# Suffix sums of a stick-breaking attention as single-pass products of a split softplus, and the adaptive units placed anew

## The chip, the cores and the metric

One core of one Trainium2 chip runs the whole kernel. The metric is device time in microseconds. Before the change three runs took 1232.63, 1235.06 and 1237.28 us, with a median of 1235.06 us. TensorE (PE in the rows; PEld is its weight load), VectorE (DVE), ScalarE (ACT), GpSimd (POOL) and SyncE (SP, which here only issues DMAs) each run a queue of instructions in order and meet at semaphores.

## The reference, cut to what matters

The kernel computes two transformer blocks on 256 tokens of width 1024. The first block is an adaptive normalisation (six vectors sh1, sc1, g1, sh2, sc2, g2 from a condition c and the weight ada_w), a stick-breaking attention of 16 heads, and a mixture of 32 experts. The second block is a feed-forward, a mixer and a feed-forward. The change is inside the attention:

```
mod = silu(c) @ ada_w + ada_b; sh1, sc1, g1, sh2, sc2, g2 = split(mod, 6)
h = rms_norm(x) * (1 + sc1) + sh1
z = q @ k.T * scale                       # per head, 256 x 256
log_keep = where(causal, log_sigmoid(-z), 0)   # = -softplus(z)
suffix = cumsum(log_keep, reverse=True) - log_keep
a = where(causal, exp(log_sigmoid(z) + suffix), 0)
x = x + g1 * ((a @ v) @ w_out)
h = rms_norm(x) * (1 + sc2) + sh2; x = x + g2 * experts(h)
```

## The kernel before

**Attention.** Heads go in pairs, p = 0 to 7. A head's logits lie transposed (keys on the partitions) in one of four PSUM banks, as 384 columns (three 128x128 blocks; the fourth is all masked), called BLK. `scores(p)` on TensorE fills the banks of the pair. ScalarE takes Abs, Exp and Ln of it (lines 1149 to 1151, tile `att_az`). VectorE's `softplus_head` (L1584) makes max(z, 0) plus that, into `att_sp`. GpSimd's `keep_causal` (L934) zeroes what is masked in the two diagonal blocks (256 columns). TensorE's `suffix_sums(p)` (L2426, L2427) adds two products to the bank of each head: `neg_ge` (a triangle of -1) times all 384 columns and `neg_ones` times the last 128 columns. Everything is plain fp32 there, and the profile shows such a product as two instructions. VectorE's `weight_logs` (L1612) copies min(sum, 0) to `att_a` and frees the bank, ScalarE takes Exp (L1159), GpSimd masks again (L934), and `weigh_values(p)` (L2436, L2440) multiplies by v. ScalarE rounds the result (L1163, `oTh`) and VectorE keeps what the rounding left (L1640, `oTl`).

**The split products.** The large projections do the same with weights and activations: a value is split into a rounded part (type fp32r, by ScalarE) and the rest (VectorE, rounded too), and three single-pass products take the place of one fp32 product (L2255 to L2257).

**The order.** Each engine's order is written out by hand as a loop over p. In iteration p TensorE does suffix_sums(p), weigh_values(p-1), one half of an adaptive unit where one is due (`ada`, L2311: SC2 in p = 1 and 2, SH2 in p = 3 and 4, G2 in p = 6 and 7), scores(p+2), and in p = 1 `gate_col` (L2334), in p = 3 and 5 `ada_col` (L2323). VectorE does weight_logs and softplus_head for two heads in turn, then `ada_part` (L1497) or `ada_col` (L1506), from p = 4 to 7 a half of an output weight's rest (`early_part`, L1538), then oTl.

**The weights' ring.** SyncE loads 2 MB units into six ring slots. The list `units_a` names them; unit n waits until unit n-6 is used. After the last of the list, the experts' weights take the same slots and five spare areas. They are again issued in order, each when its slot's last user is through: SH2's and G2's halves and the splits of the two output units release the first ones, the output products and the router the next, and the experts' own products all later ones (L804). `BankPlan` gives each PSUM use its bank.

Of the kernel before, what the change touches and what calls it, by code (L numbers as in the profile page):

```python
# [63 lines left out]
ADA_AT = {3: SC2, 5: SH2}  # L64
# [18 lines left out]
def plan_banks():  # L83
# [24 lines left out]
    for p in range(PAIRS + 2):  # L108
        if p < PAIRS:
            for h in (2 * p, 2 * p + 1):  # L110
                plan.use(("z", h), bank=h % 4, fills=2)
        if p >= 2:
            plan.use(("o", p - 2), bank=4 + p % 2, fills=0)
        if p in ADA_AT:
            plan.use(("ada", ADA_AT[p], None), bank=6, fills=0)
        if p == 2:
            plan.use(("col", G1, None), bank=7)
        if p - 1 in ADA_AT:
            plan.use(("col", ADA_AT[p - 1], None), bank=7)
    plan.use(("ada", G2, None), bank=6, fills=0)  # L120
# [96 lines left out]
def build_program(nc, x_in, c_in, ada_w, ada_b, norm_g, final_g, sb_w_in, sb_w_out, moe_w_grp, moe_b_grp,  # L217
# [5 lines left out]
    with ctx:  # L223
# [20 lines left out]
        def area(name, offset, *sizes, dt=FP32):  # L244

            return shaped(place(name, offset, [P, *sizes], dt)[0][:], sizes)
# [47 lines left out]
        att_a = area("att_a", REST + 17408, 4, BLK)  # L294

# [16 lines left out]
        neg_ones = gain0[:, 896:1024]  # L312
# [13 lines left out]
        neg_ge = vec[:, 1312:1440]  # L326
# [79 lines left out]
        def slot_b(n):  # L406
# [39 lines left out]
        z_log, z_sp, z_spm, z_a, z_am, z_o = (sem(n) for n in (  # L446
            "att_log", "att_sp", "att_sp_masked", "att_a", "att_a_masked", "att_o"))
# [102 lines left out]
        units_a += [("qkv", 2), ("qkv", 3), ("ada", G1, 0), ("ada", G1, 1), ("qkv", 4), ("qkv", 5)]  # L550
# [347 lines left out]
        def _(pool):  # L898
# [3 lines left out]
            for t, v in ((ident, 0.0), (neg_ge, -1.0), (lt, 1.0), (le, 1.0), (pick, 0.0), (strip, 0.0), (wrp, 0.0)):  # L902
                last = chain.step(g.memset(t, v))
            g.memset(neg_ones, -1.0).then_inc(consts, 1)
# [52 lines left out]
            for p in range(PAIRS + 1):  # L957
                if p < PAIRS:
                    for h in (2 * p, 2 * p + 1):
                        pool.wait_ge(z_sp, h + 1)  # L960
                        keep_causal(diag(att_sp[:, h % 4, :]), z_spm)
                if p >= 1:
                    for h in (2 * p - 2, 2 * p - 1):
                        pool.wait_ge(z_a, h + 1)
                        keep_causal(diag(att_a[:, h % 4, :]), z_am)
# [492 lines left out]
        def _(dve):  # L1458
# [147 lines left out]

            def weight_logs(g):

                b = await_full(dve, ("z", g), 2)
                if g >= 4:  # L1610
                    dve.wait_ge(z_o, g - 3)
                emptied(v.tensor_scalar(att_a[:, g % 4, :], b[:, 0:BLK], 0.0, None, ALU.min), ("z", g))  # L1612
# [6 lines left out]
            for h in range(2):  # L1619
                softplus_head(h)  # L1620
            value_copy(1, 1)
            for p in range(1, PAIRS + 2):
                for i in range(2):
                    if 1 <= p <= PAIRS:
                        weight_logs(2 * p - 2 + i)
                    if 1 <= p < PAIRS:
                        softplus_head(2 * p + i)
                if p in ADA_AT:
                    ada_part(ADA_PARTS.index((ADA_AT[p], None)))
                if p == 2:  # L1630
                    ada_col(ADA_PARTS.index((G1, None)))
                if p - 1 in ADA_AT:
                    ada_col(ADA_PARTS.index((ADA_AT[p - 1], None)))
                if 4 <= p < 8:
                    early_part(EARLY_QKV + (p - 4) // 2, p % 2)
                if p >= 2:
                    n = p - 2
                    b = bank(("o", n))
                    dve.wait_ge(oh_s, n + 1)
                    emptied(v.tensor_tensor(oTl[:, n, :], b[:, 0:T], oTh[:, n, :].bitcast(FP32), ALU.subtract), ("o", n))  # L1640
            def add_square(c):

                dve.wait_ge(sq2_s, c + 1)
                if c > 1:
                    dve.wait_ge(sq_sum_s, c - 1)
                v.tensor_tensor(sq_sum, sq_sum, sq2[:, c % 2, :], ALU.add).then_inc(sq_sum_s, 1)
# [551 lines left out]
        def _(pe):  # L2198
# [222 lines left out]
            def suffix_sums(p):  # L2421

                for g in (2 * p, 2 * p + 1):
                    b, s = bank(("z", g)), att_sp[:, g % 4, :]
                    pe.wait_ge(z_spm, g + 1)
                    t.matmul(b[:, 0:BLK], neg_ge, s, start=False, stop=True, skip_group_check=True)  # L2426
                    last = t.matmul(b[:, P:T], neg_ones, s[:, T:BLK], start=False, stop=True, skip_group_check=True)  # L2427
                    filled(last, ("z", g))
# [27 lines left out]
            for p in range(PAIRS + 1):  # L2456
# [8 lines left out]
                if 2 <= p + 1 < 6:  # L2465
                    ada(ADA_PARTS[4 + (p + 1) // 2][0], (p + 1) % 2)
                if PAIRS - 2 <= p < PAIRS:
                    ada(G2, p - PAIRS + 2)
                if p + 2 < PAIRS:
                    scores(p + 2)  # L2470
                if p == 1:
                    gate_col()
                if p in ADA_AT:
                    ada_col(ADA_PARTS.index((ADA_AT[p], None)))
# [475 lines left out]
```

## Time and profile before

| | |
|---|---|
| profiled execution | 1232.65 us |
| its span | 1230.9 us, 16444 instructions |
| PE, PEld | 1063.2 us (86%), 808.5 us (66%) |
| DVE, ACT, POOL | 510.0 us (41%), 414.3 us (34%), 71.6 us (6%) |
| attention loop | 103.82 to 146.94 us of the span |
| output projection, router | 146.94 to 188.46 us |
| experts | 188.46 to about 600 us |
| second block | about 600 us to the end |

A busy share over the whole span mixes stages with different limits, so the table says where each stage lies. The time outside the span is 1232.65 - 1230.9 = 1.75 us.

### The profile page before, as it was taken

What the parts mean: (1) busy time and instruction counts of PE and PEld (TensorE: products, weight loads), DVE (VectorE), ACT (ScalarE), POOL (GpSimd) and SP (SyncE); (2) the same over time, 40 slices, a digit from 0 to 9 for tenths busy, and PEclk for the clock granted to TensorE, in tenths of its full rate; (3) what the DMA queues carried; (4) which work ended last, traced back from release to release, by engine and by line L of the source; (5) the groups of instructions that cost most, each with busy time, mean ns of one, the idle gap of its engine ahead of it and who ended that gap; (6) DMA issues with size and microseconds to landing.
All of it is one profiled execution on the core that took longest, in us unless ns stands there. A gap on an engine that the chain in (4) does not pass through costs nothing.

```text
span 1230.9 us, 16444 instructions
## 1 busy us (share of the span) xinstructions
PE 1063.2 (86%) x7186; PEld 808.5 (66%) x7186; DVE 510.0 (41%) x617; ACT 414.3 (34%) x500; POOL 71.6 (6%) x101
## 2 busy tenths in 40 slices
PE   8999999765837383748899999999999999999998
PEld 6886693321313130313499998889888878999986
DVE  4544641120202020202075454466754886554544
ACT  3366741000100000000064444355645435434432
POOL 2073200000000000000010000000000310000000
PEclk9999999887878686969999999999999999999999
DMA  9899899999999999999996555455545346556530
GB/s 357 296 404 376 320 368 396 429 426 426 431 427 426 429 426 428 429 424 420 400 303 198 168 184 205 165 209 199 191 152 179 125 174 223 170 173 206 191 118 35
DMA packets 112822, 357.13 MB, mean 290 GB/s; under 512 B 8406, under 2 KB 55146, under 8 KB 98156
## 3 DMA queue, kind: packets, MB, share of 16 engines
q1 hardware_dynamic: 111116, 352.59, 74.1%
q10 hardware_dynamic: 1632, 3.45, 0.8%
q8 instruction: 59, 0.97, 0.3%
q14 instruction: 15, 0.12, 0.0%
HBM read 354.97 MB, written 1.05 MB: 289 GB/s over the span
## 4 chain that ended last, share of the span: by engine, by line
PE 66%; DMA 23%; SPq 5%; DVE 3%; ACT 1%; issue 1%; DVEq 0%; ACTq 0%
PE psum L2255 16%; PE psum L2257 16%; PE psum L2256 16%; DMA spare<-in_moe_w_gate_dram 5%; DMA spare<-in_moe_w_up_dram 5%; DMA ring<-in_moe_w_down_dram 5%; DMA spare<-in_moe_w_down_dram 4%; PE psum L2624 4%; PE psum L2672 3%; DMA ring<-in_moe_w_up_dram 2%; PE psum L2611 2%; DMA ring<-in_sb_w_in_dram 1%; SPq L785 1%; PE psum L2561 1%; PE psum L2311 1%
## 5 line engine op out<-in xcount | busy, mean ns | idle before, releaser
L2255 PE MATMUL psum<-hTh,wh_keep 128*128 128x256 f32 x800 | 225.4, 282 | 0.6 <-DVE hTl L1839 0.6
L2256 PE MATMUL psum<-hTl,wh_keep 128*128 128x256 f32 x800 | 224.7, 281 | 0.0
L2257 PE MATMUL psum<-hTh,wl_keep 128*128 128x256 f32 x800 | 224.7, 281 | 0.0
L1816 DVE TENSOR_TENSOR wl_stream<-ring,wh_stream 128x2048 fp32r<-128x2048 f32 x52 | 119.8, 2311 | 108.6 <-ACT wh_stream L1250 108.5
L1816 DVE TENSOR_TENSOR wl_keep<-ring,wh_keep 128x2048 fp32r<-128x2048 f32 x49 | 111.9, 2291 | 105.7 <-ACT wh_keep L1250 105.7
L2255 PEld LDWEIGHTS psum<-hTh,wh_keep 128*128 128x128 f32 x800 | 150.7, 188 | 0.9 <-issue 0.8
L2256 PEld LDWEIGHTS psum<-hTl,wh_keep 128*128 128x128 f32 x800 | 150.8, 188 | 0.0
L2257 PEld LDWEIGHTS psum<-hTh,wl_keep 128*128 128x128 f32 x800 | 150.7, 188 | 0.0
L1250 ACT ACTIVATE wh_stream<-ring 128x2048 fp32r<-128x2048 f32 x52 | 99.4, 1916 | 150.6 <-PE psum L2257 150.5
L2624 PE MATMUL psum<-spare,m_xT 128*32 128x512 f32 x416 | 90.3, 666 | 55.5 <-DMA ring<-in_moe_w_up_dram 30.3
L1250 ACT ACTIVATE wh_keep<-ring 128x2048 fp32r<-128x2048 f32 x49 | 93.6, 1919 | 124.4 <-PE psum L2257 124.0
L2624 PE MATMUL psum<-ring,m_xT 128*32 128x512 f32 x352 | 97.3, 664 | 13.4 <-DMA ring<-in_moe_w_up_dram 12.5
L2255 PE MATMUL psum<-wh_stream,hTh 128*128 128x512 f32 (+1 forms) x256 | 98.0, 383 | 0.8 <-DVE wl_stream L1816 0.8
L2257 PE MATMUL psum<-wh_stream,hTl 128*128 128x512 f32 (+1 forms) x256 | 96.4, 376 | 0.0
L2256 PE MATMUL psum<-wl_stream,hTh 128*128 128x512 f32 (+1 forms) x256 | 96.3, 376 | 0.0
L1772 DVE TENSOR_TENSOR m_h<-m_sg,psum 128x512 f32<-128x512 f32 x8 | 8.2, 1028 | 199.3 <-PE psum L2624 164.6
L2624 PEld LDWEIGHTS psum<-spare,m_xT 128*32 128x32 f32 x416 | 23.7, 122 | 96.6 <-issue 96.6
L2672 PE MATMUL psum<-ring,m_sg 128*32 128x512 f32 x288 | 54.9, 738 | 34.1 <-DMA ring<-in_moe_w_down_dram 17.7
L1202 ACT ACTIVATE m_xT<-psum,ccol 128x128 f32<-128x128 f32 x32 | 12.0, 456 | 179.8 <-PE psum L2567 179.8
L2255 PE MATMUL psum<-wh_stream,actTh 128*128 128x512 f32 x176 | 68.7, 390 | 0.0
L2256 PE MATMUL psum<-wl_stream,actTh 128*128 128x512 f32 x176 | 68.5, 389 | 0.0
L2257 PE MATMUL psum<-wh_stream,actTl 128*128 128x512 f32 x176 | 68.5, 389 | 0.0
(379 smaller groups left out, 1695.1 us busy)
## 6 DMA issues: line engine op xcount, KB each, us to landing
ring<-in_ffn_w_in_dram SPq DMA_DIRECT2D x44, 1024.0 KB, 7.8
ring<-in_moe_w_down_dram SPq DMA_DIRECT2D x18, 2048.0 KB, 37.9
ring<-in_w_mix_in_dram SPq DMA_DIRECT2D x32, 1024.0 KB, 6.3
spare<-in_moe_w_up_dram SPq DMA_DIRECT2D x14, 2048.0 KB, 34.8
ring<-in_ada_w_dram SPq DMA_DIRECT2D x24, 1024.0 KB, 13.9
ring<-in_moe_w_gate_dram SPq DMA_DIRECT2D x12, 2048.0 KB, 31.1
spare<-in_moe_w_gate_dram SPq DMA_DIRECT2D x12, 2048.0 KB, 38.9
ring<-in_moe_w_up_dram SPq DMA_DIRECT2D x10, 2048.0 KB, 37.2
```

Source lines behind the costliest of these rows:

```text
L785: sp.dma_start(dst[:, ks, :], ada_v[:, ks, lo:lo + NB]).then_inc(wa_in[n % RING_A], 16)
L1202: last = a.activation(m_xT[:, c, :], psum[:, 1, P * (c - 4):P * (c - 4) + P], ACT.Identity, scale=expert_cols[:, 0, c:c + 1], bias=expert_ ...
L1250: a.activation(dst, src, ACT.Copy).then_inc(split_h, 1)
L1816: v.tensor_tensor(split_half(h, wl), raw_half(h), split_half(h, wh).bitcast(FP32), ALU.subtract)\
L2255: t.matmul(dst, sh, mh, start=first, stop=False, skip_group_check=True)
L2256: t.matmul(dst, sh, ml, start=False, stop=False, skip_group_check=True)
L2257: return t.matmul(dst, sl, mh, start=False, stop=final, skip_group_check=True)
L2311: last = t.matmul(b[CAP * e:CAP * e + CAP, :], crep[:, 4 * s + i, :], w[:, i, NB * h:NB * h + NB], start=(s == 0 and i < 2), stop=(s == 1 ...
L2561: last = t.matmul(psum[:, c // 4, P * (c % 4):P * (c % 4) + P], hn[:, tt, P * c:P * c + P], m_sel[:, tt].rearrange("p e s -> p (e s)"), st ...
L2611: last = t.matmul(psum[CAP * e:CAP * e + CAP, 4 + i, :], m_xT[:, k, CAP * e:CAP * e + CAP], w[e // 2][e % 2][kk], start=(k == 0), stop=(k ...
L2624: last = t.matmul(psum[CAP * e:CAP * e + CAP, 4 + i, :], m_xT[:, k, CAP * e:CAP * e + CAP], w[e][:, k, :], start=(k == 0), stop=(k == KD - 1))
L2672: last = t.matmul(psum[CAP * e:CAP * e + CAP, 6 + half, :], m_hT[:, f, CAP * e:CAP * e + CAP], w[e][:, f, NB * half:NB * half + NB], start ...
```

## The change

The masked softplus is split: GpSimd masks `att_sp` in place as before, waits for itself, and copies all 384 columns into `att_sph` (fp32r, rounded). VectorE subtracts it from `att_sp` and writes the rest into `att_spl` (`softplus_rest`). `att_sph` lies where `att_az` lies and `att_spl` where `att_sp` lies, so nothing is added in memory. `neg_ge` and `neg_ones` become fp32r tiles. suffix_sums does four single-pass products per head in place of two fp32 ones, and waits for each part by itself. The adaptive units sit in other iterations, and in the ring's list the third pair of projection weights is loaded before the second half of G1.

```
-ADA_AT = {3: SC2, 5: SH2}
+ADA_UNITS = {0: (SC2, 0), 1: (SC2, 1), 2: (SH2, 0), 3: (SH2, 1), 5: (G2, 0), 7: (G2, 1)}
+ADA_COLS = {0: G1, 2: SC2, 4: SH2}
+        att_sph = area("att_sph", REST + 14336, 4, BLK, dt=F32R)
+        att_spl = area("att_spl", REST + 15872, 4, BLK, dt=F32R)
-        units_a += [("qkv", 2), ("qkv", 3), ("ada", G1, 0), ("ada", G1, 1), ("qkv", 4), ("qkv", 5)]
+        units_a += [("qkv", 2), ("qkv", 3), ("ada", G1, 0), ("qkv", 4), ("ada", G1, 1), ("qkv", 5)]
 # GpSimd, for each head of pair p
-                        keep_causal(diag(att_sp[:, h % 4, :]), z_spm)
+                        m = diag(att_sp[:, h % 4, :])
+                        chain.link(g.affine_select(out=m, in_=m, compare_op=ALU.is_gt, fill=0.0, base=0,
+                                                   pattern=[[0, 2], [1, P]], channel_multiplier=-1))
+                        g.tensor_copy(out=att_sph[:, h % 4, :], in_=att_sp[:, h % 4, :]).then_inc(z_sph, 1)
 # VectorE
+            def softplus_rest(h):
+                dve.wait_ge(z_sph, h + 1)
+                v.tensor_tensor(att_spl[:, h % 4, :], att_sp[:, h % 4, :], att_sph[:, h % 4, :].bitcast(FP32),
+                                ALU.subtract).then_inc(z_spl, 1)
             for h in range(2):
                 softplus_head(h)
+            for h in range(2):
+                softplus_rest(h)
             value_copy(1, 1)
             for p in range(1, PAIRS + 2):
                 for i in range(2):
                     if 1 <= p <= PAIRS:
                         weight_logs(2 * p - 2 + i)
                     if 1 <= p < PAIRS:
+                        if i:
+                            softplus_rest(2 * p)
                         softplus_head(2 * p + i)
-                if p in ADA_AT:
-                    ada_part(ADA_PARTS.index((ADA_AT[p], None)))
-                if p == 2:
-                    ada_col(ADA_PARTS.index((G1, None)))
-                if p - 1 in ADA_AT:
-                    ada_col(ADA_PARTS.index((ADA_AT[p - 1], None)))
+                if p - 1 in ADA_COLS:
+                    ada_col(ADA_PARTS.index((ADA_COLS[p - 1], None)))
+                if p in (2, 4):
+                    ada_part(ADA_PARTS.index((ADA_COLS[p], None)))
                 ... early_part (p = 4 to 7), oTl as before
+                if p < PAIRS:
+                    softplus_rest(2 * p + 1)
 # TensorE
-                    b, s = bank(("z", g)), att_sp[:, g % 4, :]
-                    pe.wait_ge(z_spm, g + 1)
-                    t.matmul(b[:, 0:BLK], neg_ge, s, start=False, stop=True, skip_group_check=True)
-                    last = t.matmul(b[:, P:T], neg_ones, s[:, T:BLK], start=False, stop=True, skip_group_check=True)
+                    b = bank(("z", g))
+                    for part, ready in ((att_sph, z_sph), (att_spl, z_spl)):
+                        s = part[:, g % 4, :]
+                        pe.wait_ge(ready, g + 1)
+                        t.matmul(b[:, 0:BLK], neg_ge, s, start=False, stop=True, skip_group_check=True)
+                        last = t.matmul(b[:, P:T], neg_ones, s[:, T:BLK], start=False, stop=True,
+                                        skip_group_check=True)
                     filled(last, ("z", g))
-                if 2 <= p + 1 < 6:
-                    ada(ADA_PARTS[4 + (p + 1) // 2][0], (p + 1) % 2)
-                if PAIRS - 2 <= p < PAIRS:
-                    ada(G2, p - PAIRS + 2)
+                if p in ADA_UNITS:
+                    ada(*ADA_UNITS[p])
+                elif p in ADA_COLS:
+                    ada_col(ADA_PARTS.index((ADA_COLS[p], None)))
                 if p + 2 < PAIRS:
                     scores(p + 2)
-                if p == 1:
+                if p == 0:
                     gate_col()
-                if p in ADA_AT:
-                    ada_col(ADA_PARTS.index((ADA_AT[p], None)))
+                elif p in ADA_UNITS and p in ADA_COLS:
+                    ada_col(ADA_PARTS.index((ADA_COLS[p], None)))
```

## Rows read from the trace of the kernel before

**Rows 1.** The page's first line.
```profile
span 1230.9 us, 16444 instructions
```
**Rows 2.** Windows: length, each engine's busy time (instructions), granted clock, DMA share, GB/s.
```profile
103.82:146.94 43.12, 41.78 (x306) 24.44 (x304) 25.22 (x48) 30.83 (x62) 12.64 (x30) 1.00 0.85 322
188.46:560.00 371.54, 232.52 (x1633) 86.87 (x1632) 47.90 (x87) 21.27 (x46) 0.00 (x0) 0.81 1.00 425
...
138.00:140.00 2.00, 2.00 (x17) 1.08 (x19) 2.00 (x5) 1.62 (x4) 0.04 (x1) 1.00 0.06 25
...
190.00:192.00 2.00, 2.00 (x24) 0.65 (x20) 0.00 (x0) 0.01 (x1) 0.00 (x0) 1.00 0.40 119
```
**Rows 3.** Timeline of SyncE's queue: start us, issue us, what.
```profile
141.98 2.04 SPq L753 DMA_DIRECT2D ring<-in_moe_w_up_dram  x4
...
192.12 7.14 SPq L804 DMA_DIRECT2D ring<-in_moe_w_gate_dram  x4
```
**Rows 4.** Timeline of TensorE, 103 to 118 us: start, us, what, [idle before, releaser].
```profile
103.59 0.39 PE L2257 MATMUL psum<-ewh,ehTl 128*128 128x512 f32 x1
103.82 0.81 PE L2426 MATMUL psum<-att_sp,vec 128*128 128x384 f32 x2
104.46 0.38 PE L2427 MATMUL psum<-att_sp,gain 128*128 128x128 f32 x2
104.68 0.81 PE L2426 MATMUL psum<-att_sp,vec 128*128 128x384 f32 x2
...
106.52 0.70 PE L2416 MATMUL psum<-qkT 64*128 64x256 f32 x4 [0.80 <-DVE att_a L1612]
...
107.37 0.91 PE L2426 MATMUL psum<-att_sp,vec 128*128 128x384 f32 x2
...
109.30 0.65 PE L2436 MATMUL psum<-att_a,vtok 128*64 128x256 f32 x4
...
110.10 1.92 PE L2311 MATMUL psum<-ring,gain 128*32 128x512 f32 x16
111.96 0.70 PE L2416 MATMUL psum<-qkT 64*128 64x256 f32 x4
...
114.62 0.89 PE L2426 MATMUL psum<-att_sp,vec 128*128 128x384 f32 x2
```
**Rows 5.** The chain of waits, where the loop ends.
```profile
146.14 0.58 PE psum L2436 x4
146.94 0.32 PE psum L2255
```
**Rows 6.** Timelines of ScalarE and TensorE before the loop.
```profile
74.67 1.92 ACT L1094 ACTIVATE ewh<-ring 128x2048 fp32r<-128x2048 f32 x1 [3.42 <-DMA ring<-in_sb_w_in_dram]
```
```profile
79.25 0.47 PE L2255 MATMUL psum<-ewh,ehTh 128*128 128x512 f32 x1 [0.68 <-DVE ewl L1546]
```
**Rows 7.** Timeline of all engines late in the loop.
```profile
135.15 0.70 PE L2416 MATMUL psum<-qkT 64*128 64x256 f32 x4 [0.53 <-DVE att_a L1612]
...
140.74 1.22 DVE L1538 TENSOR_TENSOR ewl<-ring,ewh 128x1024 fp32r<-128x1024 f32 x1
...
140.89 1.33 POOL L934 TENSOR_SCALAR_AFFINE_SELECT att_sp<-att_sp 128x256 f32<-128x256 f32 x1 [0.52 <-DVE att_sp L1584]
```
**Rows 8.** Single tiles and lines: duration ns min/median/max, first and last start.
```profile
L934 POOL TENSOR_SCALAR_AFFINE_SELECT att_a<-att_a x16: 402/406/408, 107.3 to 144.7; 128x256 f32<-128x256 f32 x16
```
```profile
L1584 DVE SCALAR_TENSOR_TENSOR att_sp<-psum,att_az x16: 542/548/558, 100.8 to 140.3; 128x384 f32<-128x384 f32 x16
```
```profile
L951 POOL TENSOR_TENSOR gain<-gain,ring x28: 724/740/2829, 66.1 to 95.6; 128x256 f32<-128x256 f32 x28
L1546 DVE TENSOR_TENSOR ewl<-ring,ewh x11: 2291/2293/2755, 28.9 to 149.2; 128x2048 fp32r<-128x2048 f32 x11
L1538 DVE TENSOR_TENSOR ewl<-ring,ewh x4: 1215/1226/1339, 127.1 to 140.7; 128x1024 fp32r<-128x1024 f32 x4
```
**Rows 9.** GpSimd's and ScalarE's groups by shape: count, busy us, mean ns.
```profile
L915 POOL TENSOR_SCALAR_AFFINE_SELECT le<-le 128x128 f32<-128x128 f32 x1 | 0.3, 283 | 0.0
```
```profile
L1150 ACT ACTIVATE att_az<-att_az 128x384 f32<-128x384 f32 x13 | 6.8, 523 | 0.4
```

More of the change, by code:

```diff
@@ L113, in plan_banks @@
             plan.use(("o", p - 2), bank=4 + p % 2, fills=0)
-        if p in ADA_AT:
-            plan.use(("ada", ADA_AT[p], None), bank=6, fills=0)
-        if p == 2:
-            plan.use(("col", G1, None), bank=7)
-        if p - 1 in ADA_AT:
-            plan.use(("col", ADA_AT[p - 1], None), bank=7)
-    plan.use(("ada", G2, None), bank=6, fills=0)
+        if p in ADA_UNITS and ADA_UNITS[p][1] == 0:
+            plan.use(("ada", ADA_UNITS[p][0], None), bank=6, fills=0)
+        if p in ADA_COLS:
+            plan.use(("col", ADA_COLS[p], None), bank=7)
     plan.use(("perm",), bank=7)
@@ L311, in build_program @@
         spread = gain0[:, 640:896].rearrange("p (a n) -> p a n", a=2)
-        neg_ones = gain0[:, 896:1024]
+        neg_ones = area("neg_ones", gains_at + 896, P, dt=F32R)
         adp, gate_sum = gain1.rearrange("p (a n) -> p a n", a=2), gain1
@@ L325, in build_program @@
         shift_p = vec[:, 1268:1304]
-        neg_ge = vec[:, 1312:1440]
+        neg_ge = area("neg_ge", REST + 18944 + 1312, P, dt=F32R)
         strips = vec[:, 1304:1305]
@@ L445, in build_program @@
         dve_s, act_s, pool_s = sem("dve_steps"), sem("act_steps"), sem("pool_steps")
-        z_log, z_sp, z_spm, z_a, z_am, z_o = (sem(n) for n in (
-            "att_log", "att_sp", "att_sp_masked", "att_a", "att_a_masked", "att_o"))
+        z_log, z_sp, z_sph, z_spl, z_a, z_am, z_o = (sem(n) for n in (
+            "att_log", "att_sp", "att_sp_high", "att_sp_rest", "att_a", "att_a_masked", "att_o"))
         r_diff, r_exp, r_sel, r_done = sem("rt_diff"), sem("rt_exp"), sem("rt_selected"), sem("rt_done")
@@ L901, in _ @@
             g = nc.gpsimd
-            for t, v in ((ident, 0.0), (neg_ge, -1.0), (lt, 1.0), (le, 1.0), (pick, 0.0), (strip, 0.0), (wrp, 0.0)):
+            for t, v in ((ident, 0.0), (neg_ge.bitcast(FP32), -1.0), (lt, 1.0), (le, 1.0), (pick, 0.0), (strip, 0.0), (wrp, 0.0)):
                 last = chain.step(g.memset(t, v))
-            g.memset(neg_ones, -1.0).then_inc(consts, 1)
+            g.memset(neg_ones.bitcast(FP32), -1.0).then_inc(consts, 1)
             g.memset(ones, 1.0).then_inc(consts, 1)
@@ L1626, in _ @@
                     if 1 <= p < PAIRS:
+                        if i:
+                            softplus_rest(2 * p)
                         softplus_head(2 * p + i)
-                if p in ADA_AT:
-                    ada_part(ADA_PARTS.index((ADA_AT[p], None)))
-                if p == 2:
-                    ada_col(ADA_PARTS.index((G1, None)))
-                if p - 1 in ADA_AT:
-                    ada_col(ADA_PARTS.index((ADA_AT[p - 1], None)))
+                if p - 1 in ADA_COLS:
+                    ada_col(ADA_PARTS.index((ADA_COLS[p - 1], None)))
+                if p in (2, 4):
+                    ada_part(ADA_PARTS.index((ADA_COLS[p], None)))
                 if 4 <= p < 8:
@@ L2464, in _ @@
                     weigh_values(p - 1)
-                if 2 <= p + 1 < 6:
-                    ada(ADA_PARTS[4 + (p + 1) // 2][0], (p + 1) % 2)
-                if PAIRS - 2 <= p < PAIRS:
-                    ada(G2, p - PAIRS + 2)
+                if p in ADA_UNITS:
+                    ada(*ADA_UNITS[p])
+                elif p in ADA_COLS:
+                    ada_col(ADA_PARTS.index((ADA_COLS[p], None)))
                 if p + 2 < PAIRS:
                     scores(p + 2)
-                if p == 1:
+                if p == 0:
                     gate_col()
-                if p in ADA_AT:
-                    ada_col(ADA_PARTS.index((ADA_AT[p], None)))
+                elif p in ADA_UNITS and p in ADA_COLS:
+                    ada_col(ADA_PARTS.index((ADA_COLS[p], None)))
             logits = bank(("logits",))
```

## The prediction

> **What bounds the kernel now.** I read the windows first, then SyncE's queue, then the chain, then the loop's timeline. The page's span [rows 1] hides three regimes. From 188.46 to 560 us the DMA engines are full (share 1.00, 425 GB/s) while TensorE is busy 232.52 of 371.54 us: the experts' weights bound that stage [rows 2]. Ahead of it the DMA engines still starve: at 138 to 140 us (share 0.06) and, last, at 190 to 192 us (0.40) [rows 2]. The first pause ends when SyncE issues again at 141.98 us, after VectorE's last early_part; the last one when it issues at 192.12 us, released by TensorE's first products of the experts [rows 3]. From then the stream never runs dry, so its end stands at a fixed distance behind that release, and the release follows TensorE through router, output projection and attention. So what the attention loop gains or loses on TensorE comes through whole, up to the few us of pauses that are there to be used up. In the loop TensorE is busy 41.78 of 43.12 us, VectorE 25.22, ScalarE 30.83, GpSimd 12.64 [rows 2]. TensorE bounds it, and its own idle time is two waits for weight_logs to free banks, 0.80 and 0.53 us [rows 4, 7]; by the spacing of starts they cost 0.97 (106.52 against 103.82 + 1.73) and, taken likewise, 0.61 us.
>
> **The loop's ledger before.** A pair's suffix sums take 1.93 us (107.37 to 109.30), the first pair's 1.73 us (twice 104.68 - 103.82 = 0.86). An adaptive half takes 111.96 - 110.10 = 1.86 us [rows 4]. The loop runs from 103.82 to 146.94 us [rows 4, 5], 43.1 us: 1.73 + 7 x 1.92 = 15.2 us of suffix sums, 1.6 us of those two waits, and so 26.3 us for the rest (values, scores, six adaptive halves, columns), which the change moves about and doesn't shorten.
>
> **1. The products.** An fp32 product of 384 columns takes 104.46 - 103.82 = 0.64 us, one of 128 columns 104.68 - 104.46 = 0.22 us; a single-pass product of 512 columns takes 103.82 - 103.59 = 0.23 us [rows 4]. One of 384 then takes 0.75 x 0.23 = 0.17 us. A single-pass product of 128 columns is nowhere in the trace: between 0.06 us (a quarter of 0.23) and 0.22 us (no gain over fp32). I take 0.11 us, one of the two instructions that make up the fp32 product, since its weight load is as long. A head: 2 x (0.17 + 0.11) = 0.57 us for 0.96 us. With all else hidden the suffix sums are 16 x 0.57 = 9.1 us.
> The page TensorE: Matmul & The Clock Gate of the Trainium skill (section LDWEIGHTS) gives a weight load as columns over 1.2 GHz, 107 ns for 128 columns, an estimate that would put the 128-column product at 0.11 us; the spacing of the two narrow fp32 instructions, 0.22 us for both, agrees with it [rows 4].
>
> **2. The chain to the products.** Before, a head went softplus (0.55 us), mask (0.41 us), product. Now it goes softplus, mask, wait, copy, rest, product. The mask takes 406 ns for 256 columns and 283 ns for 128 [rows 8, 9]: 0.96 ns a column over 0.16 us. A one-input copy of 384 columns by that line takes 0.53 us. Bounds: 0.41 us (as the mask) and 1.02 us (two-input adds, 740 ns for 256 columns [rows 8], by the same fixed part scaled). The rest is a two-input VectorE operation: 1226 and 2293 ns for 1024 and 2048 columns [rows 8] give 1.04 ns a column over 0.16 us, 0.56 us. With about 0.1 us at each handover the chain grows by some 1.3 us a head. Per pair VectorE gets 1.1 us more and GpSimd 1.1 us more; neither is full by sum (VectorE 25.2 + 16 x 0.48 = 33 us of 43).
>
> **3. Where the rests stand in VectorE's queue.** The rest of the even head stands behind weight_logs and holds back the odd head's softplus (0.55 us [rows 8]) until GpSimd has masked and copied. The rest of the odd head stands last, behind ada_part, the 1.22 us early_part [rows 7] and oTl, which itself waits for ScalarE. TensorE waits for it in the middle of its suffix sums, and behind that wait stand weigh_values, the adaptive half and the next scores. The bank's cycle closes there: product, weight_logs, scores, ScalarE (three passes of 0.52 us a head [rows 9]), softplus.
>
> **4. The shared port.** At 140.74 us VectorE began a two-input subtraction of 1.22 us; GpSimd's mask, begun at 140.89, took 1.33 us in place of 0.41 [rows 7, 8]. It got on only when the other was through. The other way round the subtraction of 2048 columns grew from 2291 to 2755 ns beside GpSimd's adds, which grew to 2829 from 724 [rows 8]. The rests are such subtractions, and GpSimd gets 16 copies that meet them and the early parts. I let each wait for the other, to some 0.1 us before the holder's end (1.33 us beside 0.41 says so).
> The page SBUF — State Buffer of the Trainium skill (section Who interferes with whom) calls this an exclusive lock held for the full instruction; by the trace it is let go slightly before that.
>
> **5. The walk.** I put each engine's queue in order, with these durations, and walked it through. The same walk over the kernel before ends 0.1 us from 146.94. After the change the suffix sums of pairs 0 to 7 start at 103.1, 108.8, 113.7, 119.6, 125.1, 130.5, 137.5 and 141.6 us. From start to the next product they take 1.2, 1.4, 1.5, 2.0, 2.8, 3.4, 2.5 and 4.3 us, not 1.1, plus a wait of 0.9 for pair 7's first part: 19.9 us. The last pair shows how: the softplus of head 15 runs at 142.1, early_part takes the port from 142.5 to 143.6, the mask ends 144.1, the copy 144.7, the rest 145.5, and only at 145.9 does TensorE go on to weigh_values(6) and G2's last half. Up to pair 5 the loop is ahead (adaptive halves fill the bank waits, cheap products); from pair 5 on it loses that. Sum: 19.9 - 15.2 - 1.6 = +3.1 us.
>
> **6. The ring.** The third projection unit lands one 2 MB unit earlier. Now ScalarE waits for it until 74.67 us (3.42 us idle) and through VectorE TensorE until 79.25 (0.68 us idle) [rows 6]. That idle goes and the loop starts 0.7 us earlier; what is late next is TensorE itself. G1's second half lands one unit later; GpSimd's adds of it are needed by gate_col only after 103 us. -0.7 us. SC2, SH2 are used one iteration earlier, so two output units and two expert units are requested some 6 us earlier. They only lengthen the pause before 141.98 us, since the next request still waits for the last early_part, which ends at 143.7 us by the walk. Worth nothing; nor would it cost if that cover went, the bytes being the same. gate_col in iteration 0 makes VectorE wait for it once; it is in the walk. The moved bank uses cost nothing.
>
> **Sum.** +3.1 - 0.7 = +2.4 us: the loop ends at 149.3. On the profiled execution, 1230.9 + 1.75 = 1232.65 us, it makes 1235.05; on the median of the runs, 1235.06 us, which lies 2.4 us above it, 1237.5 us. I forecast 1237.5 us.
>
> **Rivals.**
> A, TensorE stays the bound: all is hidden, 9.1 - 15.2 - 1.6 - 0.7 = -8.4 us, 1226.7 us. For it: 41.78 of 43.12 us busy, engines beside it at 25 and 31 [rows 2]. Against: what counts is the chain's length, not the sums, and a pair without an adaptive half would need 1.1 + 0.8 + 0.9 = 2.8 us of TensorE, less than the 4.3 us that VectorE's own seven operations take with an early part among them.
> B, the port doesn't matter (the collision of rows 7 was chance and the engines slip past each other): the walk without port waits ends at 147.06, +0.1 us, 1235.2 us.
> C, the copy is slow: with 1.02 us the walk ends at 154.4, +7.5 us, 1242.5 us. It decides from about 0.9 us a copy (+6). For it: two-input work costs GpSimd 2.3 ns a column; against: the mask's 0.96 ns. This is the case on the slower side in full.
> D, the 128-column single-pass product saves nothing (0.22 us): 150.5, +3.6 us, 1238.7 us; what the change says about one pass would hold for the wide half only. With both the cheap ends (0.06 and 0.41 us) it is +1.5 us.
> E, the port is held to the full end of the instruction and a little past it: the walk ends at 150.6, +3.6 us, 1238.7 us. By the Trainium skill's SBUF — State Buffer page it is this one; the 1.33 us of rows 7 speaks for the earlier release.
>
> **Chances.** The forecast 0.40, A 0.15, B 0.12, C 0.13, D 0.08, E 0.12. Plus or minus 0.5% is 6.2 us, about what a measurement of this kernel can tell. A alone lies beyond it on the fast side, and not with all its chance (0.15 less 0.04): faster 0.11. C mostly (0.11) and a little of D and E with a slower copy (0.03): slower 0.14. Same 0.75. The range leaves out the far end of A and of C: 1229 to 1243.5 us.
>
> **What would show it.** The products: L2426 once per part with about 0.17 us to the next start, and 0.11 after the narrow one. The copy: one GpSimd row per head, 0.53 us alone, longer beside L1538. The walk: TensorE idle inside suffix_sums, released by the rest on VectorE, growing from pair 3 to pair 7; the last early_part ending later than 141.98. The ring: no idle at the 79.25 product. The carry: the issue at 192.12 later by what weigh_values(7) is later by, and the DMA share at 1.00 after it. The forecast is wrong if the waits for the rests stay under 0.5 us a pair (then A), if the copy takes over 0.9 us (then C), or if a gain in the loop is not seen in the issue at 192.12.

## The result, and the profile after

The changed kernel took 1239.22 us in the median of 22 runs (1235.11 to 1242.29), the one before 1234.74 us in the median of 22 runs beside it (1232.28 to 1238.47). The ratio is 1.0032, 95% interval 1.0025 to 1.0040: 4.0 us slower, 3.1 to 4.9. The forecast was +2.4 us.

The profiled execution took 1240.75 us, 8.1 us more than the one before. That one lies 2.1 us under its kernel's median and this one 1.5 us above its own, so a single pair of traces shows about twice the difference that the runs show. Effects seen in traces are told in the traces' us; what they are worth is told in ratios.

The busy times on the page of the kernel after (TensorE hardly more than before, VectorE 7.6 us and GpSimd 12.3 us more):
```profile
PE 1064.4 (86%) x7186; PEld 808.2 (65%) x7186; DVE 517.6 (42%) x633; ACT 415.0 (33%) x500; POOL 83.9 (7%) x117
```
Windows of the kernel after, columns as in [rows 2]. The first is the attention loop, the next are 2 us slices of it, the last one is the experts' stage:
```profile
102.74:153.83 51.09, 44.50 (x305) 24.85 (x303) 32.88 (x63) 30.97 (x62) 22.28 (x44) 0.87 0.81 314
120.00:122.00 2.00, 1.42 (x12) 1.01 (x12) 1.85 (x5) 1.83 (x4) 0.00 (x0) 1.00 1.06 391
122.00:124.00 2.00, 2.00 (x16) 0.76 (x16) 1.39 (x4) 1.59 (x1) 0.91 (x2) 0.50 1.04 382
124.00:126.00 2.00, 2.00 (x14) 0.24 (x6) 0.22 (x1) 1.41 (x4) 1.63 (x4) 0.65 1.10 410
...
132.00:134.00 2.00, 0.90 (x9) 0.61 (x5) 1.79 (x5) 1.94 (x6) 1.86 (x3) 1.00 1.01 410
134.00:136.00 2.00, 1.73 (x12) 1.14 (x12) 2.00 (x4) 1.94 (x5) 1.27 (x3) 0.91 0.79 332
136.00:138.00 2.00, 2.00 (x16) 0.47 (x16) 1.39 (x4) 0.98 (x3) 0.81 (x3) 0.50 0.12 49
...
144.00:146.00 2.00, 0.71 (x4) 0.31 (x3) 2.00 (x4) 0.61 (x2) 1.21 (x1) 0.97 0.00 0
146.00:148.00 2.00, 1.26 (x4) 0.99 (x4) 1.38 (x3) 0.05 (x1) 1.65 (x4) 0.50 0.64 119
...
150.00:152.00 2.00, 2.00 (x12) 0.40 (x8) 0.42 (x1) 0.23 (x1) 0.00 (x0) 0.50 1.00 422
...
199.00:560.00 361.00, 218.84 (x1550) 81.67 (x1544) 47.45 (x86) 19.79 (x42) 0.00 (x0) 0.82 1.01 427
```
The loop runs from 102.74 to 153.83 us, 51.1 us for 43.1 [rows 2]. The loop before was granted the full clock, 1.00. This one was granted 0.87: in three stretches (122 to 125, 136 to 139, 146 to 153 us) TensorE ran at the lower of its two levels, 0.50 or 1.2 GHz, each time behind slices in which it was only partly busy (1.42, 0.90 and 0.71 of 2 us). Not every such slice has a fall behind it: from 127 to 129 us TensorE was busy for 0.89 us, and the clock stayed at 1.00 until about 135.5 us. TensorE's timeline around the first fall, columns as in [rows 4]:
```profile
119.61 0.42 PE L2441 MATMUL psum<-att_sph,neg_ge 128*128 128x384 f32 x1
...
121.24 0.44 PE L2441 MATMUL psum<-att_spl,neg_ge 128*128 128x384 f32 x1 [0.58 <-DVE att_spl L1613]
...
122.86 3.17 PE L2324 MATMUL psum<-ring,gain 128*32 128x512 f32 x16
...
129.02 0.44 PE L2441 MATMUL psum<-att_spl,neg_ge 128*128 128x384 f32 x1 [1.13 <-DVE att_spl L1613]
...
133.98 0.44 PE L2441 MATMUL psum<-att_sph,neg_ge 128*128 128x384 f32 x1 [1.10 <-POOL att_sph L964]
...
136.22 3.31 PE L2324 MATMUL psum<-ring,gain 128*32 128x512 f32 x16
```
A wait of 0.58 us for the odd head's rest, and the adaptive half behind it takes 3.17 us instead of 1.92 [rows 4]. After the waits of 1.13 and 1.10 us the next half takes 3.31 us. The loop's end, a timeline of all engines:
```profile
144.64 1.21 DVE L1541 TENSOR_TENSOR ewl<-ring,ewh 128x1024 fp32r<-128x1024 f32 x1
144.79 1.33 POOL L962 TENSOR_SCALAR_AFFINE_SELECT att_sp<-att_sp 128x256 f32<-128x256 f32 x1 [1.13 <-DVE att_sp L1587]
...
146.18 0.50 POOL L964 CAST att_sph<-att_sp 128x384 fp32r<-128x384 f32 x1
...
146.74 0.69 PE L2441 MATMUL psum<-att_sph,neg_ge 128*128 128x384 f32 x1 [1.93 <-POOL att_sph L964]
```
and the chain of waits behind it:
```profile
148.30 1.05 PE psum L2452 x4
...
149.78 3.33 PE psum L2324 x16
153.10 0.58 PE psum L2452 x4
...
153.90 0.32 PE psum L2268
```
The last early_part holds the port, GpSimd's mask takes 1.33 us, then come copy and rest, and everything that TensorE does behind them runs at 0.50: weigh_values 1.05 us for 0.58, the last half of G2 3.33. SyncE's queue afterwards, columns as in [rows 3]:
```profile
145.88 2.07 SPq L753 DMA_DIRECT2D ring<-in_moe_w_up_dram  x4
...
199.10 0.46 SPq L804 DMA_DIRECT2D ring<-in_moe_w_gate_dram  x1
```
The issue that starts the experts' stream moved from 192.12 [rows 3] to 199.10 us, +6.98, as the loop's end moved from 146.94 [rows 5] to 153.90, +6.96. From there the DMA engines are full (1.01).

### The profile page after: what moved, and what is told of

Its sections match the earlier page's. It is cut to its first block, busy times and chain, and to the rows that moved or that the text cites. A ratio compares the mean times of both kernels' runs of the same rounds, so it can differ in the third digit from the quotient of the medians.

```text
span 1238.9 us, 16476 instructions
## 1 busy us (share of the span) xinstructions
PE 1064.4 (86%) x7186; PEld 808.2 (65%) x7186; DVE 517.6 (42%) x633; ACT 415.0 (33%) x500; POOL 83.9 (7%) x117
## 3 DMA queue, kind: packets, MB, share of 16 engines
HBM read 354.97 MB, written 1.05 MB: 287 GB/s over the span
## 4 chain that ended last, share of the span: by engine, by line
PE 73%; DMA 19%; DVE 4%; ACT 1%; issue 1%; SPq 1%; POOL 1%; DVEq 0%; ACTq 0%; POOLq 0%
PE psum L2268 17%; PE psum L2270 17%; PE psum L2269 17%; DMA ring<-in_moe_w_down_dram 7%; DMA spare<-in_moe_w_down_dram 4%; PE psum L2640 4%; PE psum L2688 4%; DMA ring<-in_moe_w_up_dram 3%; DMA spare<-in_moe_w_gate_dram 2%; DMA spare<-in_moe_w_up_dram 2%; PE psum L2627 2%; PE psum L2577 2%; PE psum L2696 1%; PE psum L2324 1%; PE psum L2217 1%
## 5 line engine op out<-in xcount | busy, mean ns | idle before, releaser
L1791 DVE TENSOR_TENSOR m_xT<-psum,g2b 128x512 f32<-128x512 f32 x16 | 10.3, 686 | 140.4 <-PE psum L2688 114.4
```

## The experiments

Ratios are to the kernel before, run on the same chip. "Loop" is from the first suffix product to the first output product in the profiled run, "idle" TensorE's idle time in the timeline's rows of the loop, "clock" the granted clock of the loop's window.

| | loop us | idle | clock | experts' issue | median us | ratio (95%) |
|---|---|---|---|---|---|---|
| before | 43.1 | 1.3 | 1.00 | 192.12 | 1234.74 | |
| after | 51.1 | 6.5 | 0.87 | 199.10 | 1239.22 | 1.0032 (1.0025 to 1.0040) |
| e1_ring | 43.8 | 2.0 | 1.00 | 189.69 | 1233.11 | 0.9994 (0.9984 to 1.0004) |
| e2_place | 43.3 | 1.1 | 1.00 | 189.66 | 1231.61 | 0.9985 (0.9976 to 0.9994) |
| e3_split | 54.9 | 7.2 | 0.81 | 205.00 | 1241.96 | 1.0069 (1.0054 to 1.0084) |
| e4_high_only | 47.0 | 8.0 | 0.82 | 192.88 | 1235.23 | 1.0011 (0.9998 to 1.0024) |
| e5_busy | 46.2 | 1.5 | 1.00 | 194.08 | 1235.35 | 1.0013 (1.0003 to 1.0023) |
| e6_rest_first | 50.9 | 5.4 | 0.83 | 196.90 | 1238.24 | 1.0033 (1.0018 to 1.0048) |
| e8_place_late | 42.4 | 0.2 | 1.00 | 188.43 | 1232.18 | 0.9982 (0.9972 to 0.9993) |
| e9_busy_late | 45.6 | 1.2 | 1.00 | 191.49 | 1235.35 | 1.0012 (1.0000 to 1.0024) |
| e10_split_busy | 49.4 | 3.7 | 1.00 | 198.54 | 1239.87 | 1.0048 (1.0027 to 1.0068) |
| e11_copy_twice | 52.9 | 5.2 | 0.97 | 200.82 | 1243.14 | 1.0078 (1.0054 to 1.0102) |

In all of them the issue comes 45.2 or 45.3 us behind the loop's end. From the issue to the end of the profiled execution it is between 1040.0 us (e2_place) and 1043.0 us (e9_busy_late), so a single trace's issue foretells its time only to some 3 us. The loop's start lies anywhere from 100.6 to 104.9 us; e2, e8 and e9 share one ring order and differ by 0.56 us there, e5 and e6 share it too and start at 102.65 and 100.65. So ends are compared less safely than lengths.

### e1_ring: the new ring order alone

```diff
 # the kernel before, and
-        units_a += [("qkv", 2), ("qkv", 3), ("ada", G1, 0), ("ada", G1, 1), ("qkv", 4), ("qkv", 5)]
+        units_a += [("qkv", 2), ("qkv", 3), ("ada", G1, 0), ("qkv", 4), ("ada", G1, 1), ("qkv", 5)]
```


> The kernel before with one line of the change: the third projection unit loaded before G1's second half. Theory (the ring's order is worth about 1 us and nothing else): the 0.68 us idle ahead of the product at 79.25 goes, the loop starts about 1.1 us earlier (102.7 in place of 103.82), ratio 0.999. Rival (part of the cost comes from the ring: an early request delays a later one): the loop starts earlier but the issue behind the experts' first products is not earlier than 192.1, ratio 1.000 or above.

The idle time ahead of the loop is gone, and the loop starts 3.2 us earlier in the trace (100.67 for 103.82 us), more than the 1.1 expected; its length is as before within 0.7 us. The issue comes at 189.69 us, earlier than 192.12, so the rival is out by the trace. The ratio, 0.9994, doesn't tell the two apart: at most a small gain, and no change is inside the interval.

### e2_place: ring and placing, without the split

```diff
 # the kernel after, and
-                        g.tensor_copy(out=att_sph[:, h % 4, :], in_=att_sp[:, h % 4, :]).then_inc(z_sph, 1)
-                    for part, ready in ((att_sph, z_sph), (att_spl, z_spl)):
+                        keep_causal(diag(att_sp[:, h % 4, :]), z_sph)
+                    b, s = bank(("z", g)), att_sp[:, g % 4, :]   # neg_ge, neg_ones fp32 again; no softplus_rest
```


> The ring's order and the new placing of adaptive units, with the fp32 suffix sums of before. Theory (the cost lies in the split alone): TensorE keeps its clock at 1.00 in the loop, adaptive halves stay at 1.86 us, the loop ends near 146.2 (walk), ratio about 0.9995. Rival (the placing leaves pairs 4 and 6 short of work, TensorE waits there and its clock falls without the split too): granted clock below 1.00 in the loop, halves of 3.2 us, the loop ends at 149 or later, ratio 1.002 or above.

0.9985, faster than before and a little more so than expected (0.9995), with the loop at 43.3 us and the clock at 1.00. The cost is the split's; the placing and the ring win a little.

### e3_split: the split, with the old placing and the old ring

```diff
 # the kernel after, and ADA_UNITS, ADA_COLS, ada_part, ada_col, gate_col and units_a as before
```


> The split products alone, with the ring's order and the placing of before. Theory (chain of mask, copy, rest makes TensorE wait in every pair from 3 on; the waits then cost the clock): the walk without a change of clock ends at 151.3; with the clock at 0.5 in parts of pairs 4 to 8 it ends at 153 to 157, ratio 1.004 to 1.008. Rival (the cost is the placing's, the split is neutral): the loop ends within 1 us of 146.9, ratio 1.000.

1.0069. The loop is 54.9 us long, beyond what was expected, because the clock falls in pair 1 already. TensorE's timeline of e3_split:
```profile
109.93 0.68 PE L2445 MATMUL psum<-att_sph,neg_ge 128*128 128x384 f32 x1 [0.95 <-POOL att_sph L966]
...
112.90 3.64 PE L2328 MATMUL psum<-ring,gain 128*32 128x512 f32 x16
```
and its windows:
```profile
108.00:110.00 2.00, 1.04 (x11) 0.72 (x7) 0.92 (x3) 1.67 (x4) 1.03 (x3) 0.99 1.01 403
110.00:112.00 2.00, 2.00 (x8) 1.32 (x10) 2.00 (x4) 1.70 (x4) 1.27 (x3) 0.50 1.04 416
```
With the split the placing and the ring's order matter: 1.0069 with the old ones, 1.0032 with the new. By e1_ring the ring's share of that is small.

### e4_high_only: no rests

```diff
-                    for part, ready in ((att_sph, z_sph), (att_spl, z_spl)):
+                    for part, ready in ((att_sph, z_sph),):        # and softplus_rest is never called
```
This one leaves the rests' share out of the suffix sums.

> The changed kernel without the rests: VectorE makes none, and TensorE adds the rounded part's products alone, so the sums are those of the rounded softplus only. Theory (rests in VectorE's queue and the copies each hold TensorE up): the walk from a start at 102.7 ends at 142.6 without a change of clock; it has waits of some 2 us in pairs 4, 5 and 7, for the copy, so the clock may still fall there and the end may be up to 146. Ratio 0.995 to 0.999. Rival (the copy and the port are the whole cost, the rests are hidden): waits and clock as in the changed kernel, end at 150 or later, ratio above 1.001.

A miss: 1.0011. With half the products gone and no rest to wait for, the loop still takes 47.0 us. The timeline of e4_high_only tells why:
```profile
120.75 1.91 ACT L1097 ACTIVATE ewh<-ring 128x2048 fp32r<-128x2048 f32 x1 [3.42 <-DMA ring<-in_sb_w_out_dram]
...
124.32 1.38 PE L2446 MATMUL psum<-att_a,vtok 128*64 128x256 f32 x4 [4.28 <-POOL att_a L934]
```
and its windows:
```profile
120.00:124.00 4.00, 0.05 (x1) 0.00 (x0) 1.31 (x2) 3.25 (x5) 0.86 (x1) 0.85 1.06 390
124.00:126.00 2.00, 1.68 (x8) 1.29 (x8) 1.44 (x4) 1.91 (x5) 0.64 (x3) 0.50 1.09 437
```
The loop ran ahead of the first output unit. ScalarE's rounding of it stood ahead of an Exp in its queue and waited 3.42 us for the landing; TensorE waited 4.28 us behind it, and then the clock was at 0.50. The kernel after is at that edge already: its own rounding of that unit, at 122.41 us, waited 0.51 us for the landing. So a faster loop meets the weights there, and what the rests alone cost can't be read from this run.

### e5_busy: the same waits, with TensorE kept busy in them

```diff
+                        if (g % 2 or p == 7) and p >= (3 if part is att_spl else 5):
+                            idle = b[:, BLK:NB]            # a part of PSUM that nobody reads (for att_sph: of bank 7)
+                            for _ in range(3):
+                                t.matmul(idle, ident, ident, start=False, stop=True, skip_group_check=True)
                         pe.wait_ge(ready, g + 1)
```


> The changed kernel with three idle fp32 products of 128 columns (0.66 us) put ahead of the second part of the odd head from pair 3 on, and ahead of its first part from pair 5 on (in pair 7 both heads). They add into columns that nobody reads. Theory (TensorE's waits for the rests let its clock fall to 0.5, and that costs some 5 us of the 153.8 at which the loop ends): the clock stays at 1.00, adaptive halves take 1.86 us each, the loop ends at 148.3 to 149.5, ratio about 1.001 to 1.002. Rival (the clock's fall lies beside waits that are there anyway, the chain bounds): the clock is 1.00 but the loop still ends at 152 or later, ratio 1.003 or above.

The window of the loop of e5_busy, and its timeline where the kernel after had its first fall:
```profile
102.65:148.81 46.16, 44.61 (x366) 30.34 (x364) 32.98 (x63) 30.86 (x62) 23.23 (x44) 1.00 0.81 316
```
```profile
120.41 0.88 PE L2447 MATMUL psum<-ident 128*128 128x128 f32 x6
...
122.38 1.92 PE L2324 MATMUL psum<-ring,gain 128*32 128x512 f32 x16
...
127.46 0.44 PE L2449 MATMUL psum<-att_spl,neg_ge 128*128 128x384 f32 x1 [0.58 <-DVE att_spl L1613]
```
The rest comes just as late, the three idle products (0.7 us) fill the wait, and the adaptive half takes 1.92 us. The clock stays at 1.00, the loop is 4.9 us shorter and ends at 148.81 us. The ratio falls from 1.0032 to 1.0013, and the intervals don't overlap. Added work on TensorE made the kernel faster: the fall of the clock cost time beside the waits.

### e6_rest_first: the odd head's rest ahead of the column and the early part

```diff
+                if p < PAIRS:
+                    softplus_rest(2 * p + 1)
                 if p - 1 in ADA_COLS:
                 ...
-                if p < PAIRS:
-                    softplus_rest(2 * p + 1)
```


> The changed kernel with the rest of the odd head moved up in VectorE's queue, right behind its softplus, ahead of the adaptive copy, the output weight's part and oTl. Theory (the port and the handover to GpSimd bind, wherever the rest stands: VectorE then waits idle for the copy, and early_part and oTl come later): the walk ends 2.6 us later than that of the changed kernel, 150.9 without a change of clock; ratio 1.004 to 1.008. Rival (its place at the end of the queue is the cost): TensorE's waits for the rests go, the clock stays, the loop ends by 149, ratio 1.001 or below.

1.0033, the kernel after's own ratio, and between the two expectations. The rest is ready sooner, but VectorE stands still until GpSimd has copied, and the early part and oTl come later. TensorE now waits for the copies (3.6 us) and hardly for the rests (0.3); its idle time went from 6.5 to 5.4 us, and the clock still fell (0.83). The order of that one operation is not the point.

### e8_place_late: e2_place with the last early part after the last softplus

```diff
-                if 4 <= p < 8:
-                    early_part(EARLY_QKV + (p - 4) // 2, p % 2)
+                if p in (4, 5, 6, 8):
+                    early_part(EARLY_QKV + (p > 5), int(p in (5, 8)))
```


> The ring's order and the placing with the fp32 suffix sums, and the last half of the second output weight's rest moved from iteration 7 to iteration 8 of VectorE's loop. Theory (its collision on the shared port with the mask of head 15 costs 1.1 us at the end of the loop; pauses of the DMA engines before the last one cost nothing): the wait of 1.14 us in pair 7 goes, the loop is 42.2 us long in place of 43.3, the issue behind the experts' first products comes 1 us earlier after the same start, although the first pause of the DMA engines gets longer; ratio 0.9977. Rival (the pause counts, since that issue of expert weights comes later): no gain over 0.9985, or a loss.

The timeline of e2_place in its last pair shows the port collision that the kernel before has too [rows 7], here with a wait behind it:
```profile
138.37 1.22 DVE L1538 TENSOR_TENSOR ewl<-ring,ewh 128x1024 fp32r<-128x1024 f32 x1
...
138.52 1.33 POOL L934 TENSOR_SCALAR_AFFINE_SELECT att_sp<-att_sp 128x256 f32<-128x256 f32 x1 [1.08 <-DVE att_sp L1584]
...
139.91 0.91 PE L2430 MATMUL psum<-att_sp,vec 128*128 128x384 f32 x2 [1.14 <-POOL att_sp L934]
```
and that of e8_place_late:
```profile
138.21 0.41 POOL L934 TENSOR_SCALAR_AFFINE_SELECT att_sp<-att_sp 128x256 f32<-128x256 f32 x1 [1.08 <-DVE att_sp L1584]
...
138.67 0.91 PE L2430 MATMUL psum<-att_sp,vec 128*128 128x384 f32 x2 [0.22 <-POOL att_sp L934]
```
The mask is back at 0.41 us, TensorE's wait falls by 0.92 us and so does the loop (43.29 to 42.37 us). So in this pair the shared port's cost is shown by moving the holder away. In the time e8_place_late can't be told from e2_place: 0.9982 beside 0.9985.

### e9_busy_late: the same move in e5_busy

> The changed kernel with the idle products of e5_busy and that same move of the last half. Theory (with the clock held, the port is what is left of pair 7's wait): the loop is 1.0 us shorter than in e5_busy, 45.2 us in place of 46.2, ratio 1.0005. Rival (the chain of mask, copy and rest holds pair 7 up by itself): no change from 1.0013.

Half of it in the trace: the loop is 0.53 us shorter (46.16 to 45.63). The ratio, 1.0012 beside 1.0013, shows no gain, and the noise would hide one of that size.

### e10_split_busy: e3_split with idle products

The edit is that of e5_busy, with the idle products ahead of the odd head's second part from pair 1 on, and ahead of the first part in pairs 1, 6 and 7. They are products of 128 columns, as in e5_busy, not of 384 as the expectation has it.

> The split products alone (old placing of the adaptive halves and old ring, as in e3_split), with three idle products of 384 columns put on TensorE ahead of those suffix products that wait for a rest or a copy: ahead of the odd head's second part from pair 1 on, and ahead of the first part in pairs 1, 6 and 7. Theory (the fall of TensorE's granted clock in the loop, which follows the short waits, is what makes the split so dear with the old placing): the clock is 1.00 in the whole loop, every adaptive half takes 1.92 us, the loop is 47.5 to 49 us long where e3_split had 54.85, and the ratio to before is 1.002 to 1.004 where e3_split had 1.0069. Rival (the longer chain itself, with the halves of units in the old pairs, costs e3_split's 11 us): the loop stays over 52 us and the ratio at 1.006 or more, whatever the clock.

The loops of e10_split_busy and of e3_split, as windows:
```profile
103.90:153.28 49.38, 45.70 (x377) 31.72 (x376) 32.91 (x63) 31.19 (x62) 22.25 (x44) 1.00 0.78 294
```
```profile
104.91:159.76 54.85, 47.56 (x305) 25.77 (x304) 32.83 (x63) 31.36 (x62) 21.18 (x44) 0.81 0.67 248
```
The clock is 1.00 and the loop 5.5 us shorter: in the traces the clock costs about as much with the old placing as with the new (5.5 and 4.9 us). It is 0.4 us longer than the theory allowed, and 1.0048 lies above its 1.004; its interval overlaps e3_split's, so in the time this pair points the expected way but is not clear of the noise. The rival (the loop stays over 52 us) is out by the loop.

### e11_copy_twice: the chain made longer by one copy

```diff
 # the kernel of e5_busy, and
+                        chain.link(g.tensor_copy(out=att_sph[:, h % 4, :], in_=att_sp[:, h % 4, :]))
                         g.tensor_copy(out=att_sph[:, h % 4, :], in_=att_sp[:, h % 4, :]).then_inc(z_sph, 1)
```


> The kernel of e5_busy (clock held by idle products), with GpSimd's copy of each head's softplus made twice, the second after the first and the one that the others wait for. Theory (the chain split-copy-rest is bound to the recurrence through the queue of VectorE and the products behind it, so that each 0.5 us of it costs the loop a good part of itself in each pair): the loop grows from 46.2 to 51 to 53 us, TensorE's idle time in rows grows to 5 us or more, and the ratio to before is 1.004 to 1.008. Rival (the copy is hidden behind other work, and what the split costs is the products and VectorE's added instructions): the loop stays within 1 us of 46.2 and the ratio under 1.003.

The loop grows by 6.8 us (46.16 to 52.92), TensorE's idle time from 1.5 to 5.2 us, and the ratio to 1.0078. One clock fall came with it: from the odd head's second part in pair 1 to the next scores it is 4.65 us (110.70 to 115.35), for 3.09 in e5_busy (109.45 to 112.54), +1.56 with an adaptive half of 2.58 us in it. So some 5.2 us are the chain's, an estimate: 16 added copies of 0.5 us are 8 us, and about two thirds of them reach the loop's end. The copy is not hidden.

## Why the prediction was right, and what it missed

The direction, the size within 1.6 us and the range held. The queues, the port and the chain were right; a term for TensorE's clock was missing. That the number came so near is in part luck: the missed term, 2.3 us in the runs, is as large as the whole forecast, and it met a gain of placing and ring of 1.9 us where 0.7 was forecast. The measured time lies nearer to what D and E gave (1238.7 us) than to 1237.5, but their own rows rule both out. By its steps:

**1. The products.** A wide and a narrow product together take 0.28 to 0.29 us inside a head, as predicted, and 0.32 to 0.35 where they follow other work (0.24 at the loop's start); a head without waits takes 0.52 to 0.63 us, for 0.57. But the time is otherwise shared out. TensorE's timeline of the kernel after, first head:
```profile
102.74 0.34 PE L2441 MATMUL psum<-att_sph,neg_ge 128*128 128x384 f32 x1
102.92 0.22 PE L2442 MATMUL psum<-att_sph,neg_ones 128*128 128x128 f32 x1
102.98 0.38 PE L2441 MATMUL psum<-att_spl,neg_ge 128*128 128x384 f32 x1
103.20 0.22 PE L2442 MATMUL psum<-att_spl,neg_ones 128*128 128x128 f32 x1
```
The narrow one takes 0.06 us to the next start, not 0.11, and the wide one behind it 0.22, not 0.17. That would fit a weight load of 0.11 us that the narrow product covers for 0.06 us only, which no row shows by itself. The page TensorE: Matmul & The Clock Gate of the Trainium skill (section LDWEIGHTS) was read rightly for the load and, by these starts, wrongly for where it shows. D is out.

**2. The chain.** The lines of mask, copy and rest in the kernel after (ns min/median/max):
```profile
L962 POOL TENSOR_SCALAR_AFFINE_SELECT att_sp<-att_sp x16: 407/408/1328, 100.3 to 144.8; 128x256 f32<-128x256 f32 x16
```
```profile
L964 POOL CAST att_sph<-att_sp x16: 504/505/1376, 100.8 to 146.2; 128x384 fp32r<-128x384 f32 x16
```
```profile
L1613 DVE TENSOR_TENSOR att_spl<-att_sp,att_sph x16: 546/558/758, 101.3 to 146.7; 128x384 fp32r<-128x384 f32 x16
```
Copy 0.505 us for 0.53, rest 0.558 for 0.56. C is out. A slip without effect: VectorE's sum of 33 us took 0.48 us a rest where the sentence above it has 0.56, which makes 34; the window reads 32.88.

**3 to 5. The queue, the port and the walk.** The suffix sums of pairs 0 to 3 start at 102.74, 108.44, 113.48 and 119.61 us; predicted were 103.1, 108.8, 113.7 and 119.6. TensorE's waits inside them are released by rests and copies, as said: 0.20 us in pair 2, 0.58, 1.13 and 1.37 in pairs 3 to 5, none in pair 6, and 3.18 in pair 7, all of it for copies. The port works as read: 1.33 us beside 0.41, 1.38 beside 0.505, and VectorE's rests 0.73 beside 0.558, each let go about 0.1 us before the end of the holder's row. (VectorE's own next row starts 0.07 to 0.09 us before that end too, so part of this may lie in how the rows are drawn.)

The test of the walk is e5_busy, where the clock stayed up. Its pairs 4 to 7 start at 125.08, 130.53, 137.32 and 141.44 us, for 125.1, 130.5, 137.5 and 141.6 predicted:
```profile
125.08 0.44 PE L2449 MATMUL psum<-att_sph,neg_ge 128*128 128x384 f32 x1
...
137.32 0.44 PE L2449 MATMUL psum<-att_sph,neg_ge 128*128 128x384 f32 x1
...
141.44 0.42 PE L2449 MATMUL psum<-att_sph,neg_ge 128*128 128x384 f32 x1
```
Its loop is 46.16 us long, for 46.2 by the walk (103.1 to 149.3). So the walk's part holds, and A (all hidden) and B (no port waits, 44.0 us from the same start) are out. E (47.5 us) lies 1.3 us beyond it, and the 1.33 us speaks for the earlier release as well.

**The missed term.** From pair 4 on the measured starts of the kernel after fall behind: 126.81, 132.09, 140.31 and 143.71 us for 125.1, 130.5, 137.5 and 141.6. The walk has waits of 1 us and more on TensorE and leaves every later duration as it was; neither the sum nor a rival has a term for the granted clock. This is the step that failed: the adaptive halves were priced at 1.86 us throughout, and three of them took 3.17 to 3.4 us. The trace had a hint: the experts' stage, where TensorE is busy 232.52 of 371.54 us, runs at 0.81 [rows 2]. I read that stage for its DMA share alone. TensorE: Matmul & The Clock Gate of the Trainium skill has the case too (section A second HAM failure mode: psum-queue depth-cycling): an engine that idles briefly but often between groups of products swings between its two levels. The windows of the kernel after agree (0.50 behind slices with 1.42 and 0.71 us of work in 2), and this should have been a rival. In the traces the term is 51.09 - 46.16 = 4.9 us. In the runs it is 1.0032 - 1.0013 = 0.0019, some 2.3 us, and the noise leaves 0.8 to 3.9. The two profiled executions differ by 3.9 us (1240.75 and 1236.89): their issues are 5.0 us apart, and 1.2 us of that went in the scatter behind the issue. The profiled execution of the kernel after was no odd one, its mean clock of 0.938 being the mean of all 22 runs. So the clock's cost is shown, and its size is known only to some 2 us.

**6. The ring.** The idle time ahead of the loop is gone, and the loop starts 1.08 us earlier in the trace (0.7 predicted), within the scatter of starts. By e1_ring the ring is worth between 2.0 us of gain and 0.5 us of loss. The early requests came as said (output units at 105.91 for 112.09 us), the next request waited for the last early_part (145.88), and the longer pause, 136 to 146 us, cost nothing that shows.

**The carry.** Right as far as the issue: 45.2 or 45.3 us from the loop's end in every run, a full DMA share behind it. The distance from the issue to the end was taken as fixed and is so only within 3 us.

**The sum in ratios.** Placing and ring -0.0015 (e2_place), the split's chain with the clock held 1.0013 - 0.9985 = +0.0028, the clock +0.0019: +0.0032, or -1.9 + 3.5 + 2.3 = +4.0 us with rounding. The three add up by the way they are formed, and each is uncertain by about 0.001. Without the clock the change costs 1.6 us by e5_busy (1.0013), where the forecast, which had no clock term, said 2.4. The idle products that hold the clock cost something themselves, so the split into chain and clock is not exact.

e2_place and e8_place_late are faster than both kernels (0.9985 and 0.9982, each interval under 1).

## What to carry to other kernels

A wait put on TensorE has two prices: its length, and the clock of what follows. Where the stage before the change runs at a granted clock of 1.00 and the walk shows waits of half a microsecond and more in several pairs, add a rival in which the work behind them runs at 0.50, and test it by filling the waits with products that nobody reads. Splitting an operand saves TensorE's time only if the copy and the subtraction that make the parts don't stand in a chain that closes on TensorE: here 6 us of products were saved and paid back through VectorE's and GpSimd's queues.

## What the runs showed of the hardware

- The clock at 0.50 behind short waits: behind 0.58 us, behind 1.13 and 1.10 us, in e3_split behind 1.18 and 0.95 us. I had thought of it only for long pauses. What decides isn't settled by the length of a wait. Alone in their part of the loop, waits of 0.80 us (the kernel before), 1.18 us (e1_ring) and 1.14 us (e2_place) left the clock at 1.00. And in e11_copy_twice, with idle products beside them, waits of 1.37 and 1.32 us pass at the full clock, as its timeline and its window show.
```profile
130.06 0.44 PE L2450 MATMUL psum<-att_sph,neg_ge 128*128 128x384 f32 x1 [1.37 <-POOL att_sph L965]
...
136.92 0.45 PE L2450 MATMUL psum<-att_sph,neg_ge 128*128 128x384 f32 x1 [1.32 <-POOL att_sph L965]
```
```profile
130.00:140.00 10.00, 8.62 (x72) 6.75 (x76) 7.02 (x13) 8.22 (x15) 7.02 (x14) 1.00 0.45 185
```
- A single-pass product of 128 columns starts its successor 0.06 us later, and the 384-column one behind it takes 0.22 us to the next start, where the first of the loop took 0.18.
- More instructions on TensorE (60 idle ones in e5_busy) shortened the kernel by 0.19%.
